# Moving four weight slots off the activations' 512-byte phase in a four-layer diffusion backbone

## What is computed

```python
for i in range(DEPTH):
    m_lat, m_ctx = modulation(c), modulation(c_ctx)              # from mod_w[i]: 1024 x 6144
    h = x * (1.0 + m[1]) + m[0]
    y = mixer_i(h_lat, h_ctx)                                    # h @ w_qkv (or w_in), mixer, @ w_o
    x = layer_norm(alpha * x + m[2] * y, ln1_g[i], ln1_b[i])
    h = x * (1.0 + m[4]) + m[3]
    u = dwconv_centred(h @ ffn_w_up[i], conv_w, conv_b)          # 1024 -> 5632
    gate, val = split(u)
    f = (silu(gate) * val) @ ffn_w_down[i]                       # 2816 -> 1024
    x = layer_norm(alpha * x + m[5] * f, ln2_g[i], ln2_b[i])
return x_lat
```

## The kernel before

| moving | stationary | distance before | after |
|---|---|---|---|
| h_hi, h_lo | slab_hi, slab_lo, slots 0, 1, 2, 3 | 0, 0, 0, 0 | 128, 192, 256, 384 |
| g_hi, g_lo | slab_hi, slab_lo, slots 0, 1, 2, 3 | 448 in all | 192, 256, 320, 448 |
| slab_hi, slab_lo | h_hi, h_lo, slots 0, 1, 2, 3 | 0, 0, 0, 0 | 384, 320, 256, 128 |
| h_hi, h_lo | z_hi, z_lo (64 columns, L2099) | 320 and 64 in turn | 192 and 448 in turn |
| summed | g_first_hi, g_first_lo (L2088) | 256 and 64 | 256 and 64 |

## Time and profile before

### The profile page before, as it was taken

One profiled execution on the slowest core, in us unless ns is written; L12 is line 12 of the kernel. 1 busy time (PEld: TensorE's weight loads), 2 busy tenths in 40 slices (PEclk: granted clock), 3 DMA queues, 4 the chain that ended last, 5 costly groups with the idle time before them and its releaser, 6 DMA issues.

```text
span 2413.2 us, 35782 instructions
## 1 busy us (share of the span) xinstructions
PE 2340.2 (97%) x13872; PEld 1903.1 (79%) x13872; DVE 1696.3 (70%) x2583; ACT 1129.2 (47%) x1948; POOL 335.6 (14%) x269
## 2 busy tenths in 40 slices
PE   6999999999999989999999999899999999989998
PEld 3765888888888559888879877788888889848998
DVE  3376689988444777999875236768999845487875
ACT  3466643442442576434324444455434325386663
POOL 0000311111110003111112003422111102002110
PEclk9999999999999999999999999999999999999999
DMA  8621645557233113555563421043555645404664
GB/s 260 204 71 39 215 142 164 166 148 208 81 97 92 30 58 100 166 157 166 162 180 86 113 70 45 2 132 114 166 163 158 192 116 125 129 13 123 187 180 132
DMA packets 449420, 310.94 MB, mean 129 GB/s; under 512 B 11922, under 2 KB 404674, under 8 KB 448996
## 3 DMA queue, kind: packets, MB, share of 16 engines
q1 hardware_dynamic: 446480, 307.09, 43.2%
q10 hardware_dynamic: 2772, 1.56, 0.2%
HBM read 307.56 MB, written 1.05 MB: 128 GB/s over the span
## 4 chain that ended last, share of the span: by engine, by line
PE 85%; DVE 6%; ACT 4%; issue 2%; DMA 2%; ACTq 0%; SPq 0%; DVEq 0%
PE bank L1690 74%; PE bank L1973 2%; DMA slab_raw<-in_mod_w 2%; PE bank L1993 1%; PE bank L2037 1%; ACT p L793 1%; DVE slab_lo L1047 1%; DVE stat L1316 1%; ACT hb L610 1%; DVE q_part L1375 1%; PE bank L1749 1%; PE bank L1768 1%; ACT slab_hi L595 1%; ACT pt L805 1%; PE bank L2165 1%
## 5 line engine op out<-in xcount | busy, mean ns | idle before, releaser
L1690 PE MATMUL bank<-h_hi,slab_hi 128*128 128x512 f32 (+1 forms) x2416 | 841.9, 348 | 4.1 <-DVE h_lo L1112 2.5
L1690 PE MATMUL bank<-h_hi,slab_lo 128*128 128x512 f32 (+1 forms) x2416 | 828.9, 343 | 0.0
L1690 PE MATMUL bank<-h_lo,slab_hi 128*128 128x512 f32 (+1 forms) x2416 | 828.9, 343 | 0.0
L1047 DVE TENSOR_TENSOR slab_lo<-slab_raw,slab_hi 128x1024 fp32r<-128x1024 f32 (+1 forms) x388 | 526.2, 1357 | 296.1 <-ACT slab_hi L595 294.8
L595 ACT ACTIVATE slab_hi<-slab_raw 128x1024 fp32r<-128x1024 f32 (+1 forms) x388 | 400.8, 1034 | 303.8 <-PE bank L1690 228.0
L1690 PEld LDWEIGHTS bank<-h_hi,slab_hi 128*128 128x128 f32 x2416 | 458.0, 190 | 85.6 <-issue 19.8
L1690 PEld LDWEIGHTS bank<-h_hi,slab_lo 128*128 128x128 f32 x2416 | 458.0, 190 | 53.8
L1690 PEld LDWEIGHTS bank<-h_lo,slab_hi 128*128 128x128 f32 x2416 | 458.3, 190 | 53.3 <-issue 0.5
L1021 ACT ACTIVATE conv<-bank,prm 128x512 f32<-128x512 f32 (+1 forms) x176 | 127.7, 725 | 446.6 <-PE bank L1690 446.6
L1072 DVE SCALAR_TENSOR_TENSOR mod_sum<-slab_raw,cond_wide,mod_sum 128x512 f32<-128x512 f32 x420 | 316.5, 812 | 0.3 <-DMA slab_raw<-in_mod_w 0.2
L1690 PE MATMUL bank<-g_hi,slab_hi 128*128 128x512 f32 (+1 forms) x788 | 272.0, 345 | 0.0
(11 more groups left out here) (248 smaller groups left out, 2658.0 us busy)
## 6 DMA issues: line engine op xcount, KB each, us to landing
slab_raw<-in_ffn_w_up SPq DMA_DIRECT2D x176, 512.0 KB, 3.9
slab_raw<-in_mod_w SPq DMA_DIRECT2D x168, 512.0 KB, 4.6
slab_raw<-in_ffn_w_down SPq DMA_DIRECT2D x64, 512.0 KB, 3.6
slab_gap<-in_mod_w SPq DMA_DIRECT2D x24, 512.0 KB, 7.6
slab_raw<-in_ffn_w_down SPq DMA_DIRECT2D x32, 384.0 KB, 3.2
slab_raw<-in_b_w_qkv SPq DMA_DIRECT2D x24, 512.0 KB, 3.8
slab_raw<-in_c_w_in SPq DMA_DIRECT2D x24, 512.0 KB, 3.8
slab_raw<-in_d_w_qkv SPq DMA_DIRECT2D x24, 512.0 KB, 3.8
```

Source lines behind the costliest of these rows:

```text
L1047: nc.vector.tensor_tensor(wlo[slot][:, 0:w], raw[of][:, 0:w], whi[slot][:, 0:w].bitcast(f32), ALU.subtract).then_inc(s_lo, 1)
L1690: ins = mm(out, l, r, start=first and n == 0, stop=last and n == 2, skip_group_check=parted)
```

## The change

The slots of `slab_hi` and `slab_lo` are put at addresses 128, 192, 256 and 384 bytes (modulo 512) behind `h_hi`, with gaps of 64 to 256 bytes between them. That costs 896 bytes, by which everything behind them moves up, so that the last state tile, `state[1][1]`, no longer fits at the end. It goes behind the two `spread` tiles, into the last 1024 bytes of the region of `mod_row`, `w_gate` and `g_first_hi`, none of which is used any longer when it is written.

```diff
+SLOT_STEPS = (128, 192, 256, 384)
...
-        whi = [place(f"slab_hi{s}", [P, SLAB], f32r) for s in range(SLOTS)]
-        wlo = [place(f"slab_lo{s}", [P, SLAB], f32r) for s in range(SLOTS)]
+        def split_slots(name):
+            slots = []
+            for s in range(SLOTS):
+                top[0] += (h_at[0] + SLOT_STEPS[s] - top[0]) % 512
+                slots.append(place(f"{name}{s}", [P, SLAB], f32r))
+            return slots
+        whi, wlo = split_slots("slab_hi"), split_slots("slab_lo")
...
+        cond_at = top[0]
...
-        state = [[place(f"state{d}{s}", [P, C_HV], at=at if s < 2 else mean_at) for s in range(3)] for d in range(2)]
+        state = [[place(f"state{d}{s}", [P, C_HV], at=spread_at if (d, s) == (1, 1) else at if s < 2 else mean_at)
+                  for s in range(3)] for d in range(2)]
...
-        assert at[0] <= nc.sbuf_usable_end
+        assert at[0] <= nc.sbuf_usable_end and spread_at[0] <= cond_at
```

## The result

The changed kernel takes **2423.7 us** (median of 3 runs, 2423.54 to 2431.37), against 2409.4 before: 1.006 times as long, 95% interval 1.0042 to 1.0078. It is slower by 14.3 us; forecast was 25 us faster. The number lies within the range of 2338 to 2432, and 2.7 us from what rival 1 gave. The interval is wide: it allows 10 to 19 us. The profiled execution's span is 2421.5 us, only 8.3 us over that of before; the mean granted clock was 0.994 in it and 0.991 in the one of before, so that by an estimate (0.003 x 2413) the lower clock cost before some 7 us more.

The account below looks back on a forecast made before the run. TensorE, busy 97% of the span, was taken as the bound through the length of one matmul. The slots' -25 us, with all other terms 0, gave 2409.4 - 25 = 2384.4 us, range 2338 to 2432.

Parts of the forecast that it names:

- rival 1: 512-column matmul streams lose their one good step at distance 0 and get slower: about +12 us, 2421 us; chance 0.33.
- the 13.3 ns per matmul: Time each TensorE matmul takes beyond streaming its columns at 2.4 per ns, laid to loading the next matmul's weights.
- Does the address matter at all?: Whether operand distance changes matmul steps: yes, since one shape at one clock took 113.3, 117.8 and 120.0 ns.
- the slots' term: Matmuls at distance 0 from `h` move to the four new distances: 3.3 ns saved on each of 7824, -25 us.
- `g`: 2364 matmuls with `g` moving go from distance 448 to 192, 256, 320 and 448: 0, 5 us either side.
- Shift and state tile: Everything behind moves by 896 bytes and the state tile gets another address: 0 each, 2 us either side for the shift.
- Splits: VectorE's 1393 ns and ScalarE's 1052 ns splits get other distances; 330 ns more per split would stay hidden.
- rival 3: VectorE's splits lengthen by over 330 ns and TensorE waits in three layers' up projections: 13 us, 2422; chance 0.04.
- The limit of -80 us: Beyond a gain of about 80 us, VectorE would be next to bound the up projections of three layers.
- Rival 4: All four distances step like the 113.3 ns row: 50 us gained, 2359 us; chance 0.17 for more than 40 us.
- What would show it: Timeline signs: long `h` steps of 220 to 225 ns if right, 228 or more, unchanged or TensorE idle if wrong.

## Why the prediction was wrong

**The bound was read rightly.** TensorE's stream sets the time; 14.7 us worked out from its steps (15.7 with the short `g`) stand against 14.3 measured (10 to 19), and no other engine entered. What the 13.3 ns per matmul are stays open: the prediction laid them to the weight load of the next matmul, but half the weight columns do not make the step shorter at distance 0 (229.8 ns with 64 columns, 226.7 with 128).

**"Does the address matter at all?" was answered rightly**, against the Trainium skill's "SBUF — State Buffer", which gives TensorE two independent read ports ("Who interferes with whom") and says that it never waits on anyone ("SBUF: two separate sides"). With one stream alone on the chip the steps run from 226.7 to 234 ns for 512 columns, by the distance alone.

**The step that failed is the size and sign of the slots' term:** "I take a quarter of the 13.3 ns: two of the four slots lock as the 113.3 ns row does", for which the reason was that both slower long rows lie within 64 bytes of 0 and the change leaves that neighbourhood. The runs show the contrary. Zero is no bad neighbourhood but the best place for a long stream, 128 is among the worse ones (232.4), and 256 is 0 again, so that the four slots stand at 128, 192, 0 and 128 modulo 256. Two slots pay 5.4 to 6.2 ns a long matmul, one 2.5, one about 1, where the forecast had two gaining 6.7. The short ones gained 1.3 ns on average, not 3.3. No row of before had a long stream away from 0 that was faster; the gain was carried over from rows of 256 columns, in which alone it is real, and the same distance can be good for one length and bad for the other (64: 233.3 long, 113.3 short).

**Rival 1 was what happened**, with its mechanism and near its size: 12 us were forecast, from 2.2 to 5.8 ns on long matmuls less up to 7 us on short ones; +17.7 and -4.1 came. It had both of the only two long rows on its side, and the forecast argued them away. That was the place to give it the larger chance.

**The smaller terms held.** `g`: 0 with 5 to either side, +1.1 for the long and +1.0 for the short ones. Shift and state tile: 0, shown by the kernel with all slots at 0 (0.9997). Splits: unchanged at 1393 ns, so rival 3 did not enter. The limit of -80 us, beyond which VectorE was said to be next, does not follow from the prediction's own rows: by them VectorE covers 6.6%, more than the whole 13.3 ns, which are 104 us. Rival 4 needed the 113.3 ns step at all four distances; no long stream shows anything below 226.6.

**What would show it** named the right view: the means hid the slots, the timeline by slabs showed them, and a uniform distance does beat the four. It is 0 or 256, the old one.

## What to carry over

A row speaks for its own shape only: of two lengths of the same stream one lost and the other gained by the same move. Where a resource has a phase, a stream of it alone at each phase costs one short run and says more than three distances found by chance. A mixture of phases gives the mean of the good and the bad ones, never the best; and where moving a buffer needs a deeper wait, the price is set by what is queued behind that wait, which fell here from 3.2 us of TensorE's time to some 0.4 by three slabs.

## What was not expected of the hardware

- The step of float32r matmuls repeats with 256 bytes of distance between stationary and moving operand: 226.7 ns at 0 and 256, 232.5 at 128 and 384, 229 at 192 and 448 (512 columns).
- Even at its best, with nothing else running, such a matmul takes 13.3 ns more than 512 columns at 2.4 per ns; 384 columns at distance 0 fit the same sum, 8.32 / 48 = 173.3 ns. The Trainium skill, "TensorE: Matmul & The Clock Gate", section "Wait — 56ns, not 53.3ns?", has 215.7 ns for 512 columns; the float32r streams here never reach that, and no run here shows why. Half the weight columns change the pattern and not the level: with 64 of them the steps are 229.8 ns at 0, 232.7 at 64, 231.3 at 128 and 228.1 at 192.
- At one distance there are several steady steps (256 columns at 64 and at 192: 113.3 or 117.8 ns; 512 columns at 192: 228.8 or 233.3). In the whole kernel they are kept for hundreds of matmuls.

What stays open: why a step locks where it does, and how to choose the better lock on purpose. The order of work happens to give 113.3 to most of the short `h` in the whole kernel at distance 64, and gave it to `g` in one kernel and not in two others; a kernel that relies on it may lose it by an edit elsewhere.
